# RMS norms by halves of the tokens, interleaved with the projection panels on either side

## What is computed

```python
def rmsnorm(x, g):
    y = xf * lax.rsqrt(jnp.mean(xf * xf, axis=-1, keepdims=True) + EPS)
    return y * g
def modulate(x, g, shift, scale):
    return rmsnorm(x, g) * (1.0 + scale[:, None, :]) + shift[:, None, :]
# a sublayer of block 1, three times a layer:
x = x + gate * f(modulate(x, g, shift, scale))   # f: swiglu FFN (factor 0.5), hybrid mixer, swiglu FFN
```

## Time and profile before

| | |
|---|---|
| median of 3 runs (lowest to highest) | 4499.51 us (4498.86 to 4502.91) |
| span of the profiled execution | 4499.1 us |
| granted TensorE clock, mean over the span | 0.958 |
| PE busy / in the chain that ended last | 91% / 70% |
| DVE, ACT, POOL busy | 49%, 31%, 35% |
| DVE's share of the chain that ended last | 14% |

### The profile page before, as it was taken

The page is one execution under the profiler, slowest core; times in us unless marked ns, Lnnn a source line. Parts: engine busy times, 40 slices in busy tenths (PEclk is TensorE's granted clock), DMA queues, the critical chain, the costliest instruction groups (busy, mean ns, idle before and its releaser), DMA issues.

```text
span 4499.1 us, 55438 instructions
## 1 busy us (share of the span) xinstructions
PE 4072.7 (91%) x20125; PEld 3315.3 (74%) x20125; DVE 2189.6 (49%) x3593; ACT 1399.7 (31%) x1857; POOL 1592.1 (35%) x550
## 2 busy tenths in 40 slices
PE   5999979999999968999799988899968899998997
PEld 4888767887888756887577767578758788876885
DVE  6444755445442867563444345676753333334222
ACT  3322343223322332322333332332244422223332
POOL 2443424444443424444300002344446522234442
PEclk9999989999999989999899999899989999999998
DMA  5444423444443423442100002234414311111321
GB/s 169 144 156 146 129 72 117 145 143 138 133 156 108 118 65 122 128 156 90 30 11 10 19 1 85 79 122 145 138 59 146 117 57 49 55 55 57 93 96 54
DMA packets 529592, 439.98 MB, mean 98 GB/s; under 512 B 35932, under 2 KB 526829, under 8 KB 529197
## 3 DMA queue, kind: packets, MB, share of 16 engines
q1 hardware_dynamic: 529453, 438.11, 31.3%
HBM read 431.03 MB, written 2.83 MB: 96 GB/s over the span
## 4 chain that ended last, share of the span: by engine, by line
PE 70%; DVE 14%; issue 6%; ACT 4%; POOL 2%; SPq 1%; DMA 1%; DVEq 0%; ACTq 0%; POOLq 0%
PE ps_all L1582 18%; PE ps_all L1584 18%; PE ps_all L1583 18%; DVE acc L2028 3%; PE ps_all L1441 3%; DVE full_t L2094 2%; PE ps_all L1422 2%; DVE unit_t L2081 2%; PE ps_all L1575 1%; PE ps_all L1516 1%; PE ps_all L1530 1%; SPq L665 1%; PE ps_all L1412 1%; PE ps_all L1643 1%; PE ps_all L1427 1%
## 5 line engine op out<-in xcount | busy, mean ns | idle before, releaser
L732 POOL TENSOR_TENSOR w_lo<-raw,w_hi 128x2048 fp32r<-128x2048 f32 (+4 forms) x326 | 1341.2, 4115 | 2255.2 <-ACT w_hi L1079 2255.2
L1582 PE MATMUL ps_all<-h_hi,w_hi 128*128 128x512 f32 x2784 | 1115.7, 401 | 116.5 <-POOL h_lo L738 106.2
L1583 PE MATMUL ps_all<-h_lo,w_hi 128*128 128x512 f32 x2784 | 1098.5, 395 | 0.0
L1584 PE MATMUL ps_all<-h_hi,w_lo 128*128 128x512 f32 x2784 | 1097.7, 394 | 0.0
L1079 ACT ACTIVATE w_hi<-raw 128x2048 fp32r<-128x2048 f32 (+4 forms) x326 | 549.2, 1685 | 1646.3 <-PE ps_all L1584 1478.7
L1582 PEld LDWEIGHTS ps_all<-h_hi,w_hi 128*128 128x128 f32 x2784 | 531.5, 191 | 253.8 <-issue 91.1
L2028 DVE SCALAR_TENSOR_TENSOR acc<-g_raw,c_col,acc 128x256 f32<-128x256 f32 x1104 | 639.0, 645 | 1.7
L1584 PEld LDWEIGHTS ps_all<-h_hi,w_lo 128*128 128x128 f32 x2784 | 531.1, 191 | 115.4
L1583 PEld LDWEIGHTS ps_all<-h_lo,w_hi 128*128 128x128 f32 x2784 | 532.1, 191 | 108.2 <-issue 1.0
L1582 PE MATMUL ps_all<-hid_hi,w_hi 128*128 128x512 f32 (+1 forms) x1232 | 474.9, 385 | 29.0 <-DVE hid_lo L2115 18.9
L1584 PE MATMUL ps_all<-hid_hi,w_lo 128*128 128x512 f32 (+1 forms) x1232 | 464.9, 377 | 0.0
(11 more groups left out here) (305 smaller groups left out, 5206.9 us busy)
## 6 DMA issues: line engine op xcount, KB each, us to landing
raw<-in_w_ffn_gu_dram SPq DMA_DIRECT2D x88, 1024.0 KB, 5.0
g_raw<-in_w_mod_dram SPq DMA_DIRECT2D x72, 1024.0 KB, 5.0
raw<-in_ffn_w_in_dram SPq DMA_DIRECT2D x66, 1024.0 KB, 5.0
g_raw<-in_ada_w_dram SPq DMA_DIRECT2D x48, 1024.0 KB, 5.3
raw<-in_w_ffn_down_dram SPq DMA_DIRECT2D x32, 768.0 KB, 4.8
raw<-in_w_ffn_down_dram SPq DMA_DIRECT2D x32, 640.0 KB, 4.4
raw<-in_ffn_w_out_dram SPq DMA_DIRECT2D x24, 768.0 KB, 4.8
raw<-in_ffn_w_out_dram SPq DMA_DIRECT2D x24, 640.0 KB, 4.4
```

The lines of the kernel that those rows point to most:

```text
L732: nc.gpsimd.tensor_tensor(v(w_lo), v(raw), v(w_hi).bitcast(F32), ALU.subtract).then_inc(sem["w_split_lo"], 1)
L1582: nc.tensor.matmul(o, whi, mhi, start=first, stop=False)
L1583: nc.tensor.matmul(o, whi, mlo, start=False, stop=False)
L1584: return nc.tensor.matmul(o, wlo, mhi, start=False, stop=last)
```

## The change

The seven norms become steps of kind "rms", and the last panel of the step ahead (the "tail") moves into them.

- **Tail by halves.** PE runs the tail's last panel first for tokens 0 to 255, then for 256 to 511, with 256-column matmuls. DVE adds each half to x by itself (`add_half`). The tail keeps both banks apart (`tail_bank`).
- **Sums per token.** DVE adds the squares of the groups that are done into one tile as they come (`presum`, 6 adds of 128x512 before a dn tail, 5 before a proj tail). PE then takes the squares as weights and one column of 1/1024 as the moving operand (`sum_half`), so that each token's sum is one number on one partition. ACT takes the root of 128x2 numbers, DVE the reciprocal of 128x2, and PE spreads them over the partitions with two matmuls of 128 columns (`spread_half`). Half 0's sums and spreading stand between the matmuls of half 1 of the tail, half 1's between those of the next step's first panel.
- **Norm by half groups.** For 16 chunks (half, group) DVE makes x·scale·r into PSUM (`full`), ACT adds the shift and writes `h_hi`, DVE writes `h_lo` (`low_part`) instead of POOL. The first panel of the next step is run in 16 chunks of six 256-column matmuls (`first_panel`).
- **Moved with them.** The dn loops with sums are unrolled on PE and DVE, and in the last iteration the gemv columns of PE come ahead of the last panel. In proj the gemv columns come inside it. "mods" runs on DVE behind `add_half(0)`. ACT's `w_hi` of the next step's second panel is cut in two pieces, behind chunks 3 and 6. The root's table is loaded by a dummy ahead of the squares. In mla_in the context part of the first panel runs ahead of its latent part, and the write-back of x, with the factor of the step "alpha" folded in, follows the chunks.

```diff
...
+def rms_step(then, tail, mods, g=None):
+    n = 0 if tail is None else len(tail_of(tail))
+    tot = dict(deviation=2, r_made=2, r_spread=2, h_full=2 * KD, h_hi=2 * KD, h_ready=2 * KD)
+    if tail is not None:
+        tot.update(half_used=1, half_added=1, squared=2 * n, square_summed=2)
+    if g is not None:
+        tot.update(x_new=KD)
+    return dict(kind="rms", then=then, tail=tail, mods=mods, g=g, totals=tot)
...
-        steps += [mods_step(l * MOD_PANELS + 8, m(0), m(2), plus=[(m(1), gn(0))]),
-                  norm_step("rms_h", m(1), m(0), fused=True)] + [
+        before = steps[-1] if l else None
+        steps += [rms_step((m(1), m(0)), before, mods_step(l * MOD_PANELS + 8, m(0), m(2), plus=[(m(1), gn(0))])),
...
+    scaled = ps_all[:, 2:4, 0:HT]
+    stats = ps_all[:, 7, :], ps_all[:, 5, :]
+    dev_col, r_col, gs_col, ga_col = rstd[:, 0:4], rstd[:, 4:8], rstd[:, 8:8 + KD], rstd[:, 8 + KD:8 + 2 * KD]
...
+    def tail_bank(t, k, h):
+        bank = (5, 4)[h] if t["kind"] == "dn" else (2, 4)[h] + k - (KD - 2)
+        return ps_all[:, bank, 0:HT]
...
+        def square(h):
+            name = tail_name(tail)
+            if h == 0:
+                act.wait_ge(sem["half_added"], b["half_added"] + 1)
+            else:
+                act.wait_ge(sem[f"{name}1"], b[f"{name}1"])
+            for k in tail_of(tail):
+                nc.scalar.activation(squares.rearrange("p k n -> p (k n)")[:, half(k, h)], x[:, half(k, h)], ACT.Square).then_inc(sem["squared"], 1)
+        def deviation(h):
+            act.wait_ge(sem["square_summed"], b["square_summed"] + (h + 1 if tail else 0))
+            nc.scalar.activation(dev_col[:, 2 * h:2 * h + 2], stats[h][:, 0:2], ACT.Sqrt, bias=eps[:, 0:1]).then_inc(sem["deviation"], 1)
+        def high(n):
+            h, k = n // KD, n % KD
+            act.wait_ge(sem["h_full"], b["h_full"] + n + 1)
+            c0 = st["then"][1] + k
+            nc.scalar.activation(h_hi[:, half(k, h)], scaled[:, n % 2, :], ACT.Identity, bias=modc[:, c0:c0 + 1]).then_inc(sem["h_hi"], 1)
+        act.wait_ge(sem["consts"], 5)
+        nc.scalar.activation(rstd[:, 32:33], eps[:, 0:1], ACT.Sqrt)
+        if tail:
+            square(0)
+        deviation(0)
+        if not tail:
+            deviation(1)
+        follow = tail and ahead(tail, tail["iters"] - 1, 1, True)
+        for n in range(2 * KD):
+            high(n)
+            if tail and n == 1:
+                square(1)
+            if tail and n == 2:
+                deviation(1)
+            if tail and n in (3, 6):
+                split_hi_part(follow, n // 6)
...
+                        if st["sums"] == "square" and last and j == 1:
+                            break
...
+                pe.wait_ge(sem["h_ready"], st["pre"]["base"]["h_ready"])
+                pe.wait_ge(sem["down1"], b["down1"])
+                for bank, c0, c1, c in plans[j]:
+                    for k in range(KD):
+                        m = [t[:, k * C:(k + 1) * C] for t in (c0_hi, c0_lo)]
+                        triple(ps_d[:, 0, c * C:(c + 1) * C], whi[:, k, c0:c1], wlo[:, k, c0:c1], *m, k == 0, k == KD - 1)
+                        if c == 0 and k == 4:
+                            sum_half(st["pre"], 1)
+                        if c == 1 and k == KD - 1:
+                            spread_half(st["pre"], 1)
+                first_panel(st, [bank for bank, c0, c1, c in plans[j]]).then_inc(sem["panel_used"], 1)
+                continue
             for bank, c0, c1, c in plans[j]:
...
+            if j == 1:
+                pe.wait_ge(sem["x_new"], b["x_new"])
...
+        def sum_half(st, h):
+            b, tail = st["base"], st["tail"]
+            if h == 0:
+                pe.wait_ge(sem["pre_summed"], b["pre_summed"])
+            ks = tail_of(tail)
+            for m, k in enumerate([0] + ks):
+                if m:
+                    pe.wait_ge(sem["squared"], b["squared"] + h * len(ks) + m)
+                for t in range(2):
+                    ins = nc.tensor.matmul(stats[h][:, t:t + 1], squares[:, k, (2 * h + t) * P:(2 * h + t + 1) * P], mean_m[:, 0:1],
+                                           start=(m == 0 and t == 0), stop=(k == KD - 1 and t == 1))
+            ins.then_inc(sem["square_summed"], 1)
+        def spread_half(st, h):
+            pe.wait_ge(sem["r_made"], st["base"]["r_made"] + h + 1)
+            for t in (2 * h, 2 * h + 1):
+                ins = nc.tensor.matmul(stats[h][:, (t - 2 * h) * P:(t - 2 * h + 1) * P], r_col[:, t:t + 1].broadcast_to([P, P]), ident[:, :], start=True, stop=True)
+            ins.then_inc(sem["r_spread"], 1)
...
+            outs = tail_of(tail)
+            dn = tail["kind"] == "dn"
+            order = tuple(range(tail["nk"])) if dn else tail["order"]
+            gemvs = [] if dn else half_of(tail["gemvs"], 1)
+            at = (3, 7) if dn else (2, 4)
+            for h in range(2):
+                if h and dn:
+                    pe.wait_ge(sem["down0"], b["down0"])
+                for n, k in enumerate(order):
+                    m = [t[:, half(k, h)] for t in ((hid_hi, hid_lo) if dn else (h_hi, h_lo))]
+                    for c, out_k in enumerate(outs):
+                        cc = slice(c * P, (c + 1) * P)
+                        ins = triple(tail_bank(tail, out_k, h), whi[:, k, cc], wlo[:, k, cc], *m, n == 0, n == len(order) - 1)
+                    if h == 0 and n == 3 and len(gemvs) == 3:
+                        reduce_gemv(gemvs[1])
+                    if h == 1 and n == 0 and len(gemvs) > 1:
+                        reduce_gemv(gemvs[-1])
+                    if h == 1 and n == at[0]:
+                        sum_half(st, 0)
+                    if h == 1 and n == at[1]:
+                        spread_half(st, 0)
+                ins.then_inc(sem["panel_used" if h else "half_used"], 1)
+        def first_panel(st, banks, j=0):
+            pre = st["pre"]
+            nb = pre["base"]
+            whi, wlo = (w_view(t, j, st["shapes"][j]) for t in (w_hi, w_lo))
+            for h in range(2):
+                for k in range(KD):
+                    n = h * KD + k
+                    mhi, mlo = (t[:, half(k, h)] for t in (h_hi, h_lo))
+                    outs = [b_[:, h * HT:(h + 1) * HT] for b_ in banks]
+                    pe.wait_ge(sem["h_hi"], nb["h_hi"] + n + 1)
+                    for c, o in enumerate(outs):
+                        cc = slice(c * P, (c + 1) * P)
+                        nc.tensor.matmul(o, whi[:, k, cc], mhi, start=(k == 0), stop=False)
+                        nc.tensor.matmul(o, wlo[:, k, cc], mhi, start=False, stop=False)
+                    pe.wait_ge(sem["h_ready"], nb["h_ready"] + n + 1)
+                    for c, o in enumerate(outs):
+                        ins = nc.tensor.matmul(o, whi[:, k, c * P:(c + 1) * P], mlo, start=False, stop=(k == KD - 1))
+                    if pre["tail"] and st["kind"] != "mla_in" and n == 1:
+                        sum_half(pre, 1)
+                    if pre["tail"] and st["kind"] != "mla_in" and n == 4:
+                        spread_half(pre, 1)
+            return ins
...
+        def add_half(h):
+            name = tail_name(tail)
+            if h == 0:
+                dve.wait_ge(sem["half_used"], b["half_used"] + 1)
+            else:
+                dve.wait_ge(sem["panel_used"], tail["p0"] + 2 * tail["iters"])
+            for k in tail_of(tail):
+                v, g = x[:, half(k, h)], tail["gate"] + k
+                ins = V.scalar_tensor_tensor(v, tail_bank(tail, k, h), modc[:, g:g + 1], v, ALU.mult, ALU.add)
+            ins.then_inc(sem[f"{name}1" if h else "half_added"], 1)
+        def turn_over(h):
+            dve.wait_ge(sem["deviation"], b["deviation"] + h + 1)
+            V.reciprocal(r_col[:, 2 * h:2 * h + 2], dev_col[:, 2 * h:2 * h + 2]).then_inc(sem["r_made"], 1)
+        def full(n):
+            h, k = n // KD, n % KD
+            if k == 0:
+                dve.wait_ge(sem["r_spread"], b["r_spread"] + h + 1)
+                if tail and h:
+                    dve.wait_ge(sem[f"{tail_name(tail)}1"], b[f"{tail_name(tail)}1"])
+            if n >= 2:
+                dve.wait_ge(sem["h_ready"], b["h_ready"] + n - 1)
+            s_ = gs_col[:, k:k + 1] if st["g"] is not None else modc[:, scale + k:scale + k + 1]
+            V.scalar_tensor_tensor(scaled[:, n % 2, :], x[:, half(k, h)], s_, stats[h][:, 0:HT], ALU.mult, ALU.mult).then_inc(sem["h_full"], 1)
+        def low_part(n):
+            h, k = n // KD, n % KD
+            dve.wait_ge(sem["h_hi"], b["h_hi"] + n + 1)
+            V.scalar_tensor_tensor(h_lo[:, half(k, h)], scaled[:, n % 2, :], modc[:, shift + k:shift + k + 1], h_hi[:, half(k, h)].bitcast(F32),
+                                   ALU.add, ALU.subtract).then_inc(sem["h_ready"], 1)
+        if tail:
+            add_half(0)
+        if st["mods"] is not None:
+            mods_dve(st["mods"], dve, ch)
+        if st["g"] is not None:
```

(32 more changed lines are left out.)

171 lines of the change are left out of this document (124 added, 47 removed).

## The result

| | before | changed |
|---|---|---|
| median (lowest to highest), 4 runs each | 4499.18 us (4496.21 to 4502.91) | 4432.18 us (4427.76 to 4436.11) |
| span of the profiled execution | 4499.1 us | 4434.3 us |
| ratio of the times | | 0.9844, 95% interval 0.9829 to 0.9859 |

The forecast was 4422 (4396 to 4456); the change gives 67 us where 77 were forecast. Two later sets of runs gave 4435.5 and 4431.5 for the changed kernel.

A forecast was written before the change was run, and what follows sets the result against it. PE, busy 91% of the span, was taken as the bound, with holes at the norms. Gains of 33.9 + 9.8 + 8 + 24.3 + 9.2 = 85.2 us, less 6 and 2, gave 77.2: 4499.1 to 4422, range 4396 to 4456.

The forecast's parts named there:

- The chunk's pitch: First panels behind the norms: DVE paces the sixteen chunks with `full` and `low_part`, 0.91 us a chunk.
- rival A: First panels: `full` and `low_part` stretch beside POOL's `w_lo` despite the PSUM operand; 25 us lost, 4447; chance 0.16.
- the adds of squares: Tails: DVE's adds, two SBUF inputs, stretch to POOL's end; without stretching, -3 us at five places, 4407.
- Rival B: First panels and tails: PE, waiting between chunks, stays at 1.2 GHz; 53 us lost, 4475; chance 0.07.
- place 4: Norm behind a down projection with a gemv: panel ends at 33.5 instead of 43.4; gain 11.3 us with sums.
- place 7: Norm with x's write-back: context part runs while the norm starts, 59.9 us becomes 37; gain 24.3 with sums.
- Place 1: Norm without a tail: shorter norm, but PE starts cold at half clock; 91.2 us becomes 82, gain 9.2.
- Places 3 and 6: Norms behind output projections (proj tails), where PE waits for gemvs and half 0's sums: gains 9.8 and 8 us.
- The spell: TensorE at half clock behind holes of 1.5 to 3.6 us at six places: 1 us each, 6 given back.
- Place 5: Norm behind a down projection without a gemv: PE waits some 3.3 us for squares; end 33.9, gain 11.3.
- The mixers: Two mixers: DVE's convolution has 0.5 us slack and DVE leaves the norm later; 1 us each given back.
- Rival E: First panels: a chunk is a ring through three engines without overlap, 1.55 to 1.75 us; 4516 at 1.75; chance 0.04.

The follow-up runs named there:

- the tile in SBUF: Changed kernel with the tile between `full` and `low_part` in SBUF instead of PSUM: 4465.7 us.
- the kernel with four pieces: Changed kernel with ACT's `w_hi` split in four pieces behind chunks 3, 5, 7 and 9 instead of two: 4436.0 us, the changed kernel beside it 4435.5.
- the squares' edits: Changed kernel with ACT's last squares ahead of its weight split at four down projections: 4426.1 and 4425.6 us; with mods also ahead of `add_half(0)`: 4418.6.
- the experiment on half 1's order: Changed kernel with the last gemv's columns and half 0's sums later in half 1 of the proj tails: 4428.9 us, the changed kernel beside it 4431.5.
- the edit that frees them, with mods: Changed kernel with ACT's squares ahead of its weight split and mods ahead of `add_half(0)` at four down projections: 4418.6 us.
- two new orders of PE: Changed kernel with half 0's sums and spreading behind the tail: 4432.6 us; with gemv columns and those sums later in half 1 of proj tails: 4428.9.

## Why the prediction was right, and where it missed

**Right.** What bounds the kernel, and what the change removes: the wait for `h_lo` of block 1 went from 71.5 us to nothing. (The forecast put all 106.2 us of that line down to these norms and expected them gone; 34.6 of them belong to the second stack and stayed, which its sum did not use.) The chunk's pitch (0.91 forecast and measured) and that DVE paces it: `low_part` starts 0.40 behind `full`, the next `full` 0.51 behind `low_part`, so one of the two meetings overlaps and the other costs about 0.03, as the sum had it. That operands in PSUM keep `full` and `low_part` clear of POOL (rival A), shown from both sides, by the rows above and by the tile in SBUF. That the adds of squares stretch to POOL's end (4.69). Rival B (half clock through the first panels): at place 4 the clock stays at 1.00. Place 4 was forecast at 10.3 net and gave 10.0, in other parts: the last products came at 35.1 behind the gemv columns instead of 33.5, 0.4 of it ahead of the first `full` and 1.1, as I read it, from ACT's pieces of `w_hi` behind chunks 3 and 6, which I had left to the upper bound (cut in four they gave back only 0.4); the iteration without PE's sums gave 1.8 instead of 1.4; and no slow spell came. PE stood only 0.45 us for the add of squares, for 1.5 forecast.

**Missed: three terms of the sum.** By the trace the change gives 12.4 us less than the 77.2 of the sum, and 10 less by the medians. Of the 12.4, 8.1 stand at three places. Another 2.2 stand behind place 7, where one trace of the changed kernel has 1.2 the other way, so they are chance as far as is known.

*Place 1* (3.1): the term was 82 for the panel's end, and it was 85.1. With place 4's 15.7 us from the first `full` to the last product (17.8 to 33.5), 82 puts the first `full` at 66.3; it stands at 69.62. So it is the norm's head that was priced too low, and the forecast gave no sum for it. PE, the rows up to the first product:

```profile
64.19 3.55 PE L1809 MATMUL ps_all<-mean_m,squares 128*128 128x1 f32 x16
68.36 2.08 PE L1708 MATMUL ps_all<-ident,rstd 128*128 128x128 f32 x8 [0.62 <-DVE rstd L2000]
70.77 0.55 PE L1762 MATMUL ps_all<-h_hi,w_hi 128*128 128x256 f32 x1 [0.33 <-ACT h_hi L858]
```

Sixteen one-column matmuls 0.21 apart and eight spreading ones 0.24 apart are twice the 0.10 to 0.12 that they need at place 4. Fourteen and a half us of chunks follow the first `full`.

*Places 3 and 6* (3.1 and 1.9). The head was right: half 0's add stands at 23.6 behind the start of the last two panels (forecast 24.3), the first `full` at 28.5. But from there the end took 19.5 and not the 15.7 of place 4's sum, some 2.2 of it because `add_half(1)` stands behind the second `full` on DVE and waits for the tail's end, which at a proj tail is 18 matmuls away and not 6. (A second output group to add costs 0.4, and two waits for ACT's `h_hi` behind the first piece of `w_hi` cost 1.35.) DVE at place 3:

```profile
682.54 0.48 DVE L2017 SCALAR_TENSOR_TENSOR h_lo<-ps_all,modc,h_hi 128x256 fp32r<-128x256 f32 x1
684.74 0.88 DVE L1995 SCALAR_TENSOR_TENSOR x<-ps_all,modc,x 128x256 f32<-128x256 f32 x2 [1.72 <-PE ps_all L1778]
```

And there PE is slow just then; the same four microseconds in stretches of the changed kernel, PE never idle at a granted clock of 0.57:

```profile
680.40:684.40 4.00, 4.00 (x23) 4.00 (x22) 1.36 (x3) 0.87 (x2) 0.00 (x0) 0.57 0.09 28
```

The spell was in the forecast at 1 us a place, and its price turned out to depend on when it falls and how long it lasts. In the kernel with four pieces the spell at this place comes 6 us later, when PE would wait between chunks anyway, and the place takes 1.6 less:

```profile
679.20:684.40 5.20, 4.83 (x41) 4.63 (x39) 2.98 (x8) 1.48 (x4) 0.00 (x0) 1.00 0.24 77
686.10:690.20 4.10, 4.10 (x24) 4.00 (x24) 3.10 (x8) 3.21 (x8) 0.00 (x0) 0.61 0.00 0
```

In another trace of the changed kernel it lasts three times as long, and the place takes 1.6 more:

```profile
675.30:685.50 10.20, 9.18 (x43) 8.80 (x42) 3.91 (x11) 4.39 (x9) 0.00 (x0) 0.50 0.62 204
```

The traces with the same order of work at place 3 fall into line with this. The changed kernel gains 5.8 there in the two traces with a spell of 3.4 us and 4.3 in the one with 10.2; the three traces of the squares' edits alone, all with 10.2, gain 4.2 to 4.3. Place 6 goes the same way: 4.5 where the spell is 6.8 us long, 1.4 to 1.6 where it is 13.7. So this much of what wanders between executions is the length and place of the spells. At place 3 the long spell costs 1.6 more than the short one, and the short one some 1.2 more than a late one (the four pieces give 0.4 of the 1.6 by themselves, as at places 2 and 4). The rest of the miss is argued to be the longer tail's; the experiment on half 1's order does not settle it, as its spell was 10.2.

*Place 5* (0.9): its end is given as 33.9 in the forecast, with place 4's 11.3 all the same; by the forecast's own 33.9 the term is 10.9.

*The mixers* gave back 1.1 and 0.5, for 1 each. *The adds of squares* cost PE 6.7 us of waits; the edit that frees them, with mods, shows that this wait and the delay behind it were worth 9.4.

*Rival E* had its mechanism right and its size wrong: the ring costs 1.42 a chunk, and three quarters of the difference reach the end.

## What to carry to other kernels

When a norm is cut into pieces that feed matmuls, look first at the order of its two halves on the engine that paces it; one position was worth 42 of 67 us here. Keep one operand in PSUM wherever POOL runs beside it (some 30 us here); and of the rest, find what stands first behind each long POOL instruction, since freeing one handed the stretch to the next here, however small it was. Before an order is changed to fill a hole, ask what ends the hole: two new orders of PE changed the median by less than 3 us. And before two traces are compared at one place, compare the granted clock there.

## What the runs showed of the hardware

- A DVE multiply of 128x8 took 0.17 us, 2.80 and 3.72, the latter two with both tensor inputs in SBUF while POOL ran one instruction of 4.6 us. POOL's ended at 1061.39 and the multiply of 2.80 at 1061.42: the stretch is the rest of POOL's instruction, not a factor. An add of 128x512 (0.68 by itself) took 4.69 in the same way, and a 128x256 `low_part` with both inputs in SBUF 4.44 for 0.48.
- At place 1 of the changed kernel PE ran at half pace (0.213 between 256-column matmuls up to 72.8, 0.12 behind) while the granted clock of the profile read 1.00. The spacing of equal matmuls is the safer reading.
- At place 3 a spell of TensorE at a granted clock of 0.50 came in every trace of the changed kernel, and lasted 3.4 us in two and 10.2 in the third, at different microseconds. The long one made the place 1.6 us longer.
